# A fused trunk layer on one core: the DeltaNet scan's steps in another order on all engines, and prompt attention with paired value products and four buffers of turned weights

## The chip, the cores and the metric

The kernel is one program on one core of a Trainium2 chip. The engines are TensorE (PE, with its weight loads shown as PEld), VectorE (DVE), ScalarE (ACT), GpSimd (POOL) and SyncE (SP), which here only issues transfers. The metric is the time of one execution in device microseconds. Everything is float32, or float32 split into a rounded part and a rest (names with `hi` and `lo`).

## What is computed

One layer for two groups of frames: a prompt of 1024 frames and a sample of 32 frames of a running stream, model width 1024. Cut from the reference:

```python
def gated_delta_rule(q, k, v, g, beta, s0):        # 8 heads of 64, blocks of 64 positions
    ...
    a_mat = jnp.where(strict, jnp.einsum('nbhid,nbhjd->nbhij', kb, kc) * decay, 0.0)
    sol = lax.linalg.triangular_solve(a_mat + jnp.eye(l, dtype=a_mat.dtype), rhs,
                                      left_side=True, lower=True, unit_diagonal=True)
    ...
    def step(s, xs):
        v_new = u_i - jnp.einsum('bhld,bhde->bhle', w_i, s)
        o = (jnp.einsum('bhld,bhde->bhle', q_i * jnp.exp(g_i)[..., None], s)
             + jnp.einsum('bhij,bhje->bhie', qk_i, v_new))
        s = (s * jnp.exp(g_last)[..., None, None]
             + jnp.einsum('bhld,bhle->bhde', k_i * jnp.exp(g_last[..., None] - g_i)[..., None], v_new))
        return s, o

def stick_breaking_block(q, k, v, q_pos, k_pos):   # 8 heads of 64, queries in blocks of 128
    z = jnp.einsum('bqhd,bshd->bhqs', q, k).astype(jnp.float32) * SB_SCALE
    log_keep = jnp.where(valid, jax.nn.log_sigmoid(-z), 0.0)
    log_rest = lax.cumsum(log_keep, axis=3, reverse=True) - log_keep
    a = jnp.where(valid, jnp.exp(jax.nn.log_sigmoid(z) + log_rest), 0.0)
    return jnp.einsum('bhqs,bshd->bqhd', a.astype(v.dtype), v)
```

Before these stand a norm and one input projection, with a short convolution on the DeltaNet columns; after them an output projection, a squared-ReLU MLP of width 4096, and a gated embedding.

## The kernel before

The stages follow each other: projections; prompt attention (from about 430 us of the span to 615); attention of the 32 sample frames over a cache of 2048 (to 648); the DeltaNet scan (to 919); then the output projection, MLP and embedding, which are dense products on PE. Every engine has an instruction order written out by hand in its own block, and waits on counted semaphores. An engine never skips a waiting instruction, so the order in each block is a part of the schedule.

**Prompt attention** runs 64 steps `y`: four pairs of heads, eight blocks of 128 queries, two heads (`u`) of the pair. A step's width is 128 x (block number + 1) keys, 128 to 1024. For step `y` PE makes `scores`, ACT `sigmoids` (two passes), DVE a running product from the right (`tensor_tensor_scan`, L1544) and a product (L1545), PE turns the weights block by block (`turn_weights`, L1941), ACT copies them out of PSUM into `turned_buf` (`copy_weights`, L1146), and PE multiplies them with the values (`values`, L1954). Before, `values(y)` uses 128 value columns as the stationary operand for each head although a head needs 64, so half of each result is not used; two halves, one of each head, are then copied and split by two ACT instructions (`round_out`, L1139) and two DVE instructions (`rest_of_out`, L1533) of 64 partitions. At step `y` the order on PE is `scores(y+3)`, `turn_weights(y+1)`, `values(y)`, and on ACT `sigmoids(y+3)`, `copy_weights(y+1)`, `round_out`.

**The scan** handles 9 chunks `q`: chunk 0 is the sample (one block of 64 positions), chunks 1 to 8 are 128 prompt frames each (two blocks `g`). For each chunk, without the state: the squares and norms of q and k (`squares`, `square_sums` L2116, `logs`, `inverse_norms`, `unit_norms` L1593), the decay matrices (`raw_differences` and `decays` on POOL, `decay_differences` L1585 on DVE, `decays` on ACT), the key and query products (`key_products`, `query_products`, L2125, drained by `key_matrix` and `query_matrix`), and the inverse of the triangular matrix. This inverse starts with the 16x16 diagonal blocks: `at_out` writes the matrix to DRAM (before, `blocks_out`), `lanes_in` reads its diagonal blocks back with one block per partition, DVE inverts all of them at once (`lanes_begin`, `lanes_middle`, `lanes_end`, L1642 and L1646), SP writes them to DRAM twice (`lanes_out`, L768 and L769) and reads them back in matrix form (`t_in` L774, `x_in_blocks` L779; before, all four in `blocks_in`). PE then joins them to 32 and 64 (`first_matrices` L2219, `first_inverse` L2227 and L2233, `second_matrices`, `second_inverse`), with ACT copies between (`first_masks`, `first_blocks`, `second_masks`, `second_blocks`). The part with the state is a chain for each block: `keys_on_state` (L2163), `rest_of_values`, `solved_values` (L2172), `new_values`, `state_change` (L2181), `new_state`, and beside it `outputs` (L2193, L2197). The output is squared, summed, normed, gated, turned (`turn_outputs`, L2208), rounded and split.

Each engine has a loop over `i` in which it handles several chunks at different stages. Before, `first_matrices(i+1)` stands right behind `keys_on_state(i, 0)` on PE, the lanes of chunk `i+2` stand between the two state steps of chunk `i` on DVE, and SP waits inside `blocks_in` and `blocks_out` for one transfer to land before it issues the next. `heads_part` puts parts of the first output tile into the last iterations.

SP's `sums_in`, `conv_qk_in`, `conv_v_in` and `z_in` load a chunk's decays, q and k, v, and gate. `split_ring` on POOL splits the dense stages' weight blocks.

## Time and profile before

| | |
|---|---|
| median of 3 runs | 1903.82 us (1903.76 to 1904.57) |
| profiled execution | 1903.72 us, of it span 1902.0 us |
| PE busy | 1738.7 us, 91% of the span |
| DVE busy | 767.2 us, 40% |
| ACT busy | 502.4 us, 26% |
| POOL busy | 615.0 us, 32% |
| mean granted TensorE clock | 0.962 |

Busy time of PE is the time in which at least one matrix product was under way; it says little of how full the array was. The granted clock is a share of 2.4 GHz: 1.00 is 2.4 GHz, 0.50 is 1.2 GHz, and a number between is a mean over time.

### The profile page before, as it was taken

The page shows a single profiled execution, that of the slowest core. Times are in us where ns is not written, and L with a number is a line of the kernel's source. Part 1 is how long each engine was busy: PE and PEld are TensorE (multiplying, and loading weights), DVE is VectorE, ACT ScalarE, POOL GpSimd, SP SyncE. Part 2 cuts the span into 40 slices and gives each one's busy share as a digit, 9 for nine tenths or more (in the row PEclk, how much of TensorE's full clock was granted, in tenths as well). Part 3 has the DMA queues.
Part 4 walks back from the last instruction along what each step waited for, and adds up shares of the span by engine and source line. Part 5 has one row for each costly group of instructions (what it writes and reads, how often), then busy time and mean ns, then how long its engine had stood idle before and what let it go on. Part 6 is the DMA issues. An engine that isn't in the chain of part 4 may idle for free.

```text
span 1902.0 us, 33199 instructions
## 1 busy us (share of the span) xinstructions
PE 1738.7 (91%) x14512; PEld 1648.3 (87%) x14512; DVE 767.2 (40%) x988; ACT 502.4 (26%) x970; POOL 615.0 (32%) x340
## 2 busy tenths in 40 slices
PE   4999999997999756776999999999999999999998
PEld 4989989995777446666999999999999999999898
DVE  5552134547998455664125222122212222216422
ACT  5222103226776533342113101010100000003211
POOL 4231331322332022212433434343434444432520
PEclk9999999998999878787999999999999999999999
DMA  5112321114000534333231111111111111112211
GB/s 173 46 46 68 105 63 59 68 57 131 1 1 1 155 83 98 86 64 79 65 89 45 45 45 45 45 45 45 46 54 45 45 45 45 45 45 68 56 56 48
DMA packets 202662, 116.50 MB, mean 61 GB/s; under 512 B 74448, under 2 KB 196764, under 8 KB 202524
## 3 DMA queue, kind: packets, MB, share of 16 engines
q1 hardware_dynamic: 193024, 101.45, 18.9%
q10 hardware_dynamic: 9500, 13.02, 1.9%
q8 instruction: 111, 1.82, 0.4%
q14 instruction: 27, 0.22, 0.0%
HBM read 92.60 MB, written 21.84 MB: 60 GB/s over the span
## 4 chain that ended last, share of the span: by engine, by line
PE 73%; DVE 13%; DMA 4%; issue 4%; ACT 2%; SPq 2%; POOL 1%; ACTq 0%; DVEq 0%; POOLq 0%
PE psum L2090 42%; PE psum L1902 8%; PE psum L2376 5%; DVE act_lo_plain L1544 3%; PE psum L1871 3%; PE psum L1872 3%; PE psum L1873 3%; DVE act_hi_plain L1545 2%; DVE area L1642 1%; DMA area<-x_scratch 1%; DMA x_scratch<-area 1%; PE psum L1954 1%; PE psum L2395 1%; DVE area L1482 1%; DVE area L1646 1%
## 5 line engine op out<-in xcount | busy, mean ns | idle before, releaser
L2090 PE MATMUL psum<-act_hi,w_round 128*128 128x352 f32 x1920 | 367.6, 324 | 0.3 <-DVE act_lo L1774 0.3
L940 POOL TENSOR_TENSOR w_round<-w_plain,ones 128x1024 fp32r<-128x1024 f32 x80 | 175.6, 2194 | 508.4 <-DMA w_plain<-in_w_up_dram 227.8
L2090 PEld LDWEIGHTS psum<-act_hi,w_round 128*128 128x128 f32 x1920 | 319.8, 188 | 1.3 <-DVE act_lo L1774 0.6
L2090 PE MATMUL psum<-hid_hi,w_round 128*128 128x352 f32 x1344 | 257.5, 323 | 0.4 <-DVE hid_lo L1804 0.4
L2090 PEld LDWEIGHTS psum<-hid_hi,w_round 128*128 128x128 f32 x1344 | 222.4, 188 | 0.7 <-DVE hid_lo L1804 0.7
L1781 DVE TENSOR_TENSOR area<-psum,area 128x1056 f32<-128x1056 f32 x72 | 90.5, 1257 | 307.6 <-PE psum L2090 307.6
L2090 PE MATMUL psum<-act_lo,w_round 128*128 128x352 f32 x960 | 206.7, 323 | 0.0
L941 POOL TENSOR_TENSOR w_round<-w_plain,w_round 128x1024 fp32r<-128x1024 f32 x80 | 197.7, 2472 | 6.3
L1401 ACT ACTIVATE hid_hi<-area 128x1056 fp32r<-128x1056 f32 x28 | 30.4, 1087 | 589.1 <-DVE area L1797 589.1
L1871 PE MATMUL psum<-w_round,act_hi 128*128 128x256 f32 (+1 forms) x576 | 165.8, 288 | 6.8 <-POOLq L890 3.6
L2090 PEld LDWEIGHTS psum<-act_lo,w_round 128*128 128x128 f32 x960 | 163.2, 188 | 0.0
L1872 PE MATMUL psum<-w_round,act_hi 128*128 128x256 f32 (+1 forms) x576 | 163.1, 283 | 0.0
L1873 PE MATMUL psum<-w_round,act_lo 128*128 128x256 f32 (+1 forms) x576 | 162.0, 281 | 0.0
L2090 PE MATMUL psum<-hid_lo,w_round 128*128 128x352 f32 x672 | 143.9, 323 | 0.0
L1797 DVE SCALAR_TENSOR_TENSOR area<-psum,area 128x1056 f32<-128x1056 f32 x32 | 40.2, 1258 | 239.6 <-PE psum L2090 234.7
L887 POOL TENSOR_TENSOR w_round<-w_plain,ones 128x2048 fp32r<-128x2048 f32 x14 | 50.5, 3610 | 256.1 <-PE psum L1873 165.3
L2090 PEld LDWEIGHTS psum<-hid_lo,w_round 128*128 128x128 f32 x672 | 113.8, 188 | 0.0
L1871 PEld LDWEIGHTS psum<-w_round,act_hi 128*128 128x128 f32 (+1 forms) x576 | 104.0, 181 | 8.4 <-ACTq L1067 4.0
L1902 PE MATMUL psum<-act_hi,w_round 128*128 128x352 f32 x576 | 109.1, 324 | 0.0
L1873 PEld LDWEIGHTS psum<-w_round,act_lo 128*128 128x128 f32 (+1 forms) x576 | 104.4, 181 | 0.5
L1872 PEld LDWEIGHTS psum<-w_round,act_hi 128*128 128x128 f32 (+1 forms) x576 | 103.9, 180 | 0.5
L1544 DVE TENSOR_TENSOR_SCAN act_lo_plain<-act_lo_plain,w_plain 128x128 f32<-128x128 f32 (+7 forms) x64 | 88.3, 1380 | 24.2 <-ACT act_hi_plain L1133 14.2
(295 smaller groups left out, 2705.7 us busy)
## 6 DMA issues: line engine op xcount, KB each, us to landing
w_plain<-in_w_up_dram SPq DMA_DIRECT2D x32, 512.0 KB, 4.0
w_plain<-in_w_down_dram SPq DMA_DIRECT2D x32, 512.0 KB, 3.4
w_plain<-in_w_in_dram SPq DMA_DIRECT2D x14, 1024.0 KB, 5.4
conv_scratch<-area ACTq DMA_DIRECT2D x12, 512.0 KB, 2.7
area<-in_x_prompt_dram SPq DMA_DIRECT2D x8, 512.0 KB, 3.6
w_plain<-in_cache_k_dram SPq DMA_DIRECT2D x4, 1024.0 KB, 5.3
w_plain<-in_w_out_dram SPq DMA_DIRECT2D x8, 512.0 KB, 5.6
w_plain<-in_x_prompt_dram SPq DMA_DIRECT2D x8, 512.0 KB, 4.8
```

Of the source, the lines that this page charges most:

```text
L887: own.link(pool.tensor_tensor(hi, w_raw[:, slot, :], ones[:, 0:1].to_broadcast([P, BLK]), ALU.mult))
L940: own.link(pool.tensor_tensor(hi, ring_raw(n), ones[:, 0:1].to_broadcast([P, RB]), ALU.mult))
L941: pool.tensor_tensor(lo, ring_raw(n), hi.bitcast(F32), ALU.subtract).then_inc(ring_split, 1)
L1544: own.link(dve.tensor_tensor_scan(back, back, starts, 0.0, ALU.mult, ALU.max))
L1781: dve.tensor_tensor(h3, chunks_of(bank_set(tile)), h3, ALU.add).then_inc(drained, 1)
L1797: dve.scalar_tensor_tensor(out=by_chunk(wide[:, n % 2, :]), in0=chunks_of(bank_set(tile)), scalar=0.0, in1=by_chunk(wide[:, 2, :]), op0=AL ...
L1871: pe.matmul(out, hi[:, k, cols], w_h(k), start=(k == 0), stop=False)
L1872: pe.matmul(out, hi[:, k, cols], w_l(k), start=False, stop=False)
L1873: last = pe.matmul(out, lo[:, k, cols], w_h(k), start=False, stop=(k == K - 1))
L1902: last = pe.matmul(bank(base + c)[0:rows, 0:CH], w(k), a[:, k, CH * c:CH * (c + 1)], start=(k == 0 and w is lhs_hi and a is hi), stop=(k = ...
L2090: last = pe.matmul(bank(bank_set(tile) + c)[:, 0:CH], w(k), a(k)[:, CH * c:CH * (c + 1)], start=(begins and k == ks[0] and w is w_h and a ...
L2376: last = pe.matmul(bank(c)[:, 0:CH], w(k), a[:, k, CH * c:CH * (c + 1)], start=(k == 0 and w is w_h and a is act_hi), stop=(k == KT - 1 an ...
```

## The change

In prompt attention `values` is called once for two steps. For each block of keys it makes two products, one for each head, each with 64 value columns as the stationary operand, into the lower and the upper 64 partitions of one 128x128 result. `round_out` and `rest_of_out` become one instruction of 128 partitions each. `turned_buf` has four buffers in place of two; the new ones lie in `w_plain` where `d_cqk` and `d_gb` of the scan lie, so `conv_qk_in(0)` and `sums_in(0)` are issued after the last value product of the stage.

In the scan the order of the steps in all five loops is new. Per chunk every engine has the same instructions as before. The lanes are handled one iteration earlier against the state steps (chunk `i+3` in DVE's iteration `i`, chunk `i+2` before), SP's two long helpers are cut into five that are interleaved, and `outputs(i, 1)` stands before `state_change(i, 1)`. Of the diff, the removed loops are left out (the listing above has them):

```diff
-        turned_buf = (act_hi_plain[:, DEEP * TP:(DEEP + 1) * TP], act_lo_plain[:, DEEP * TP:(DEEP + 1) * TP])
+        turned_buf = (act_hi_plain[:, DEEP * TP:(DEEP + 1) * TP], act_lo_plain[:, DEEP * TP:(DEEP + 1) * TP],
+                      w_plain[:, 2 * BLK:2 * BLK + TP], w_plain[:, 2 * BLK + TP:2 * BLK + 2 * TP])
         q_stage = carve(area, tok0 + 2 * SW + 2 * TP + 5 * P, 2, P)
...
             conv_v_in(1)
             sp.wait_ge(consts_made, 5)
             for scratch in (at_all, x_all, t_all):
                 sp.dma_start(scratch, zeros).then_inc(scratch_cleared, 16)
             sp.wait_ge(g_stored, 16)
-            sums_in(0)
             sp.wait_ge(kc_turned, 2)
             cache_keys_in(2)
+            sp.wait_ge(o_ready, 1 + STEPS // 2)
+            conv_qk_in(0)
+            sums_in(0)
             sp.wait_ge(kc_turned, 4)
             cache_keys_in(3)
...
                 sp.wait_ge(z_stored[u], 16 * NTT)
             sp.dma_start(d_sin[:, 0], state_of["in"]).then_inc(s_loaded, 16)
 
...
+            def at_out(q):
                 sp.wait_ge(at_made, q + 1)
                 for u in range(2):
                     sp.dma_start(at_scratch[u, 0:HD, 0:mats(q)], d_at[HD * u:HD * (u + 1), q % 3, 0:mats(q)])\
                       .then_inc(at_dumped, 16)
+
+            def lanes_in(q):
                 sp.wait_ge(at_dumped, 32 * (q + 1))
                 if q:
                     sp.wait_ge(scattered, 32 * q)
                 sp.dma_start(d_lane[:, 0:LB * LB].rearrange("l (r c) -> l r c", c=LB), at_lanes).then_inc(gathered, 16)
 
...
+            def lanes_out(q):
                 sp.wait_ge(lanes_made, q + 1)
+                if q:
+                    sp.wait_ge(blocks_back[(q - 1) % 2], 64 * ((q - 1) // 2 + 1))
                 sp.dma_start(t_lanes, d_lane_t.rearrange("l (r c) -> l r c", c=LB)).then_inc(scattered, 16)
                 sp.dma_start(x_lanes, d_lane[:, 0:LB * LB].rearrange("l (r c) -> l r c", c=LB)).then_inc(scattered, 16)
+
+            def t_in(q):
                 sp.wait_ge(scattered, 32 * (q + 1))
                 if q >= 2:
                     sp.wait_ge(m_ready, level(q - 2, 1))
                 for u in range(2):
                     sp.dma_start(d_t[HD * u:HD * (u + 1), q % 2, 0:mats(q)], t_scratch[u, 0:HD, 0:mats(q)])\
                       .then_inc(blocks_back[q % 2], 16)
+
+            def x_in_blocks(q):
                 if q >= 3:
                     sp.wait_ge(vn_ready, steps_to(q - 3))
                 for u in range(2):
                     sp.dma_start(d_x[HD * u:HD * (u + 1), q % 3, 0:mats(q)], x_scratch[u, 0:HD, 0:mats(q)])\
                       .then_inc(blocks_back[q % 2], 16)
...
+            def at(q):
+                return 0 <= q < CHUNKS
+
+            for i in range(-3, CHUNKS + 1):
+                if i >= -1 and at(i + 2):
+                    sums_in(i + 2)
+                if at(i):
+                    t_in(i)
+                if at(i + 1):
+                    lanes_in(i + 1)
+                if at(i):
+                    x_in_blocks(i)
+                if i == CHUNKS - 1:
+                    for done in (kg_made, qg_made, qry_ready, kv_turned, cn_made):
+                        sp.wait_ge(done, CHUNKS)
+                    for n in range(DN_RING, RING):
+                        ring_in(n)
+                if at(i - 1):
+                    if i == 1:
                         sp.wait_ge(consts_made, 6)
...
+                    z_in(i - 1)
+                if i == 3:
                     sp.wait_ge(s_new, 2)
                     sp.dma_start(state_of["sample"], d_sin[:, 1]).then_inc(s_stored, 16)
...
+                if i >= -2 and at(i + 3):
+                    conv_qk_in(i + 3)
+                if at(i + 1):
+                    lanes_out(i + 1)
+                if at(i + 2):
+                    at_out(i + 2)
+                if i >= -1 and at(i + 3):
+                    conv_v_in(i + 3)
...
+            def at(q):
+                return 0 <= q < CHUNKS
+
+            for i in range(-2, CHUNKS + 1):
+                if at(i + 2):
+                    raw_differences(i + 2)
+                if at(i - 1):
+                    decay_state(i - 1, 0)
+                if at(i - 1) and i > 1:
+                    decay_state(i - 1, 1)
+                if at(i + 2):
+                    decays(i + 2)
+                if at(i + 1):
+                    decayed_keys(i + 1)
+                if i >= CHUNKS - 2:
...
                 act.activation(sig_buf[:, n, 0:w], z, ACT.Sigmoid, scale=HD ** -0.5).then_inc(sig_made, 1)
 
             def round_out(t):
-                act.wait_ge(o_ready, 1 + 2 * t + 2)
+                act.wait_ge(o_ready, 1 + t + 1)
                 k, cols = WT + t // NT, slice(P * (t % NT), P * (t % NT + 1))
-                for u in range(2):
-                    last = act.activation(act_hi[half(u), k, cols], bank(6 + t % 2)[half(u), P * u:P * (u + 1)], ACT.Copy)
-                last.then_inc(o_rounded, 1)
+                act.activation(act_hi[:, k, cols], bank(6 + t % 2)[:, 0:P], ACT.Copy).then_inc(o_rounded, 1)
 
             def copy_weights(y):
                 w = P * (y % UNITS // 2 + 1)
                 act.wait_ge(att_turned, 1 + y + 1)
-                act.wait_ge(o_ready, 1 + earlier(y, 2))
-                act.activation(turned_buf[y % 2][:, 0:w], psum[:, 4:6, :].rearrange("p b c -> p (b c)")[:, 0:w],
+                if y >= 4:
+                    act.wait_ge(o_ready, 1 + y // 2 - 1)
+                else:
+                    act.wait_ge(dense_ready, NC)
+                act.activation(turned_buf[y % 4][:, 0:w], psum[:, 4:6, :].rearrange("p b c -> p (b c)")[:, 0:w],
                                ACT.Copy).then_inc(att_placed, 1)
 
             for y in range(DEEP):
...
                 act.activation(rs, rs, ACT.Exp, scale=-0.5).then_inc(norms_made, 1)
 
             def last_decays(q):
-                act.wait_ge(diff_made, q + 1)
+                act.wait_ge(dtb_made, 2 * q + 1)
...
                     act.wait_ge(qt_made, q - 1)
+                    act.wait_ge(kd_made, q - 1)
+                act.wait_ge(diff_made, q + 1)
                 act.activation(d_dt[:, q % 2, 0:mats(q)], d_db[:, 0:mats(q)], ACT.Exp).then_inc(dt_made, 1)
...
+                return 0 <= q < CHUNKS
+
+            for i in range(-4, CHUNKS + 1):
+                if at(i):
+                    second_blocks(i)
+                if at(i - 1):
+                    output_norms(i - 1)
+                if at(i + 1):
+                    turned_values(i + 1)
+                if at(i + 2):
+                    last_decays(i + 2)
+                if at(i + 3):
+                    logs(i + 3)
+                if at(i + 1):
                     first_masks(i + 1)
...
+                if at(i + 3):
+                    inverse_norms(i + 3)
+                if at(i + 2):
+                    state_decays(i + 2)
+                if at(i + 3):
+                    decays(i + 3)
+                if at(i + 1):
                     first_blocks(i + 1)
...
+                if at(i + 4):
+                    squares(i + 4)
+                if at(i - 1):
+                    rounded_output(i - 1)
+                if at(i + 1):
                     second_masks(i + 1)
...
+                if at(i):
+                    output_squares(i)
             act.wait_ge(s_stored, 32)
...
-                for u in range(2):
-                    last = dve.tensor_tensor(act_lo[half(u), k, cols], bank(6 + t % 2)[half(u), P * u:P * (u + 1)],
-                                             act_hi[half(u), k, cols].bitcast(F32), ALU.subtract)
-                last.then_inc(o_split, 1)
+                dve.tensor_tensor(act_lo[:, k, cols], bank(6 + t % 2)[:, 0:P], act_hi[:, k, cols].bitcast(F32),
+                                  ALU.subtract).then_inc(o_split, 1)
...
+            def at(q):
+                return 0 <= q < CHUNKS
+
+            for i in range(-4, CHUNKS):
+                if i > 0:
                     new_state(i, 1)
...
+                if at(i):
+                    output_sums(i)
+                if at(i + 1):
+                    rest_of_values(i + 1, 0)
+                if at(i + 3):
+                    query_matrix(i + 3)
+                if at(i):
+                    normed_output(i)
+                if at(i + 1):
+                    new_values(i + 1, 0)
+                if at(i + 4):
+                    decay_differences(i + 4)
+                if at(i):
+                    gated_output(i)
+                if at(i + 3):
+                    lanes_begin(i + 3)
+                if at(i + 1):
+                    new_state(i + 1, 0)
+                if at(i + 3):
+                    lanes_middle(i + 3)
+                if at(i + 4):
+                    unit_norms(i + 4)
+                if at(i + 3):
+                    lanes_end(i + 3)
+                if at(i + 1) and i >= 0:
+                    rest_of_values(i + 1, 1)
+                if at(i + 4):
+                    key_matrix(i + 4)
+                if at(i + 2):
+                    first_transposed(i + 2)
+                if at(i + 1) and i >= 0:
+                    new_values(i + 1, 1)
+                if at(i + 3):
                     decayed_queries(i + 3)
...
-            def values(y):
-
-
-                i, u, t = y // UNITS, y % 2, y // 2
-                pe.wait_ge(att_placed, 1 + y + 1)
-                if u == 0:
-                    pe.wait_ge(o_split, 1 + max(t - 1, 0))
+            def values(t):
+
+                i = t // NT
+                pe.wait_ge(att_placed, 1 + 2 * t + 2)
+                pe.wait_ge(o_split, 1 + max(t - 1, 0))
                 for n in range(t % NT + 1):
                     rows = P - 1 if n == t % NT else P
-                    last = pe.matmul(bank(6 + t % 2)[:, P * u:P * (u + 1)], v_tok[0:rows, n, P * i:P * (i + 1)],
-                                     turned_buf[u][0:rows, P * n:P * (n + 1)], start=(n == 0), stop=(n == t % NT))
+                    for u in range(2):
+                        first = P * i + HD * u
+                        last = pe.matmul(bank(6 + t % 2)[half(u), 0:P], v_tok[0:rows, n, first:first + HD],
+                                         turned_buf[(2 * t + u) % 4][0:rows, P * n:P * (n + 1)], start=(n == 0), stop=(n == t % NT))
...
                 pe.wait_ge(qt_made, q + 1)
+                pe.wait_ge(vn_made, n + 1)
                 if q:
                     pe.wait_ge(on_read, q)
                 for k in range(WT):
...
+                last_ks, final = i == CHUNKS - 2, i == CHUNKS - 1
+                if at(i + 1):
                     first_inverse(i + 1)
...
+                if at(i) and i > 0:
                     keys_on_state(i, 1)
                 if final:
+                    heads_part([WT + 2], False)
+                if at(i - 1):
+                    turn_outputs(i - 1)
+                if at(i + 3):
+                    key_products(i + 3)
+                if at(i + 2):
+                    turn_keys(i + 2)
+                if at(i) and i > 0:
+                    solved_values(i, 1)
+                if final:
+                    heads_part([WT + 3], False)
+                if at(i + 1):
+                    second_matrices(i + 1)
+                if at(i) and i > 0:
+                    outputs(i, 1)
+                    state_change(i, 1)
+                if at(i + 1):
+                    second_inverse(i + 1)
+                    keys_on_state(i + 1, 0)
+                if last_ks:
+                    pe.wait_ge(m_made, level(i + 1, 1))
+                    pe.wait_ge(qt_made, CHUNKS)
+                    pe.wait_ge(x_made, level(i + 1, 1))
+                    heads_part([WT], True)
+                if at(i + 3):
+                    query_products(i + 3)
+                if at(i + 1):
+                    solved_values(i + 1, 0)
+                if last_ks:
                     heads_part([WT + 1], False)
...
+                if at(i + 4):
+                    square_sums(i + 4)
+                if at(i + 2):
+                    first_matrices(i + 2)
+                if at(i + 1):
+                    state_change(i + 1, 0)
+                    outputs(i + 1, 0)
             def turn_x(m):
                 pe.wait_ge(x_loaded[0], 16 * (NTT // 3) + 16 * (m + 1))
                 if m:
```

## Rows read from the trace of the kernel before

**Rows 1.** The page: granted TensorE clock in 40 slices of 47.6 us, in tenths.

```profile
PEclk9999999998999878787999999999999999999999
```

**Rows 2.** Windows of the prompt attention; window, its length, then busy time of each engine.

```profile
482.40:525.05 42.65, 41.02 (x264) 31.57 (x265) 38.93 (x49) 32.76 (x70) 15.75 (x17) 1.00 0.01 2
525.05:568.00 42.95, 41.18 (x264) 31.59 (x264) 39.23 (x49) 31.36 (x65) 16.62 (x17) 1.00 0.00 1
...
439.00:482.40 43.40, 35.39 (x201) 27.02 (x201) 35.76 (x36) 28.54 (x47) 7.80 (x11) 0.88 0.36 114
```

**Rows 3.** Groups by shape in 430 to 625: busy us, mean ns, idle before.

```profile
L1533 DVE TENSOR_TENSOR act_lo<-psum,act_hi 64x128 fp32r<-64x128 f32 x64 | 18.5, 289 | 7.2 <-ACT act_hi L1139 6.0
```

**Rows 4.** Timeline of the attention: start, duration, instruction, in brackets idle before it.

```profile
467.60 2.02 DVE L1544 TENSOR_TENSOR_SCAN act_lo_plain<-act_lo_plain,w_plain 128x896 f32<-128x896 f32 x1 [2.39 <-ACT act_hi_plain L1133]
...
525.98 1.95 PE L1954 MATMUL psum<-act_hi_plain,area 128*128 128x128 f32 x16
...
526.18 1.02 ACT L1146 ACTIVATE act_lo_plain<-psum 128x1024 f32<-128x1024 f32 x1 [0.96 <-PE psum L1941]
...
529.09 0.69 DVE L1544 TENSOR_TENSOR_SCAN act_lo_plain<-act_lo_plain,w_plain 128x256 f32<-128x256 f32 x1 [0.83 <-ACT act_hi_plain L1133]
...
531.42 0.69 DVE L1544 TENSOR_TENSOR_SCAN act_lo_plain<-act_lo_plain,w_plain 128x256 f32<-128x256 f32 x1 [1.18 <-ACT act_hi_plain L1133]
```

**Rows 5.** Timeline of the cache attention, PE: products into parts of the partitions.

```profile
620.68 1.08 PE L2011 MATMUL psum<-act_hi_plain,y_sample_t 128*64 128x512 f32 x4
...
626.04 0.65 PE L2039 MATMUL psum<-w_plain,act_hi_plain 128*32 128x64 f32 x32
```

**Rows 6.** The chain that ended last, in the scan: start, duration, what.

```profile
689.48 0.61 SPq L768
...
762.60 0.60 DVE area L1585
...
764.04 0.45 DVE area L1642 x2
...
769.98 0.60 SPq L768
...
775.24 3.15 DMA area<-x_scratch
...
778.43 2.00 PE psum L2219 x32
...
786.35 0.47 PE psum L2193 x16
...
787.28 1.91 PE psum L2116 x4
...
880.04 0.60 SPq L768
...
918.15 0.70 DVE act_lo L1725
```

**Rows 7.** Waits of the SP queue in 680 to 880: us in total, times, longest.

```profile
SPq L768 <- DVE w_plain L1678: 63.0, 7, 10.2
```

**Rows 8.** Windows of the scan, columns as in rows 2, then clock and DMA share.

```profile
734.73:844.51 109.78, 80.06 (x1926) 71.85 (x1928) 65.34 (x145) 42.54 (x97) 21.91 (x20) 0.78 0.38 85
...
771.00:772.50 1.50, 0.00 (x0) 0.00 (x0) 1.50 (x3) 0.00 (x0) 0.00 (x0) 0.96 0.64 73
...
784.50:786.00 1.50, 1.50 (x34) 1.50 (x34) 0.39 (x1) 0.28 (x2) 0.00 (x0) 0.50 0.73 156
786.00:787.50 1.50, 1.50 (x43) 1.43 (x41) 1.07 (x4) 0.79 (x3) 0.60 (x1) 0.99 0.54 132
```

**Rows 9.** Timeline of one cycle of the scan, DVE and the SP queue.

```profile
772.01 1.20 DVE L1593 TENSOR_TENSOR area<-w_plain 128x1024 f32<-128x1024 f32 x1
...
804.83 1.27 SPq L758 DMA_DIRECT2D at_scratch<-area  x2
...
810.41 2.14 SPq L671 DMA_DIRECT2D w_plain<-decay_scratch  x2
```

147 lines of the change are left out of this document (13 added, 134 removed).

## The prediction

> **What bounds the kernel now.** I read the page's slices first. The granted clock is at 2.4 GHz nearly everywhere and lower only in slices 10 to 20, which are the two stages of this change and the one between them [rows 1]. The rest is dense product work that the diff does not touch, so I price only these stages and let everything behind them move up.
>
> *Prompt attention.* Its four groups of 16 steps take 43 us each. In a window of one group PE is busy 41.0 to 41.2 us and DVE 38.9 to 39.3 us [rows 2]: both are nearly full, and ACT at 31 to 33 us is not. The chain of waits and the timeline say who is last where. Inside a group DVE runs without a gap; at the change from width 1024 back to 128 DVE idles, and the last two idle pieces are 0.83 and 1.18 us while ACT and PE are late [rows 4]. A group therefore costs DVE's own work and some 3 us of stall. The first group has a third kind of time: 2.39 us in which DVE waits while PE is behind at the lower clock [rows 4], and busy sums of 35 us in 43 [rows 2].
>
> *The scan.* The chain is one repeated cycle. DVE's decay differences and lanes (762.60 to 769.98), SP's issues and transfers to x landing at 778.39, then PE's first matrices, inverse and the rest of its queue, until DVE may go on [rows 6]. From the lanes of chunk 1 done (689.48) to those of chunk 8 (880.04) there are seven cycles: 190.6 / 7 = 27.2 us each. In four cycles of 109.78 us the busy sums are 80.1 for PE (at a mean clock of 0.78), 65.3 for DVE, 42.5 for ACT and 21.9 for POOL [rows 8]: per cycle DVE has 16.3 us of work, ACT 10.6, POOL 5.5. No engine is full; the cycle is set by latency. SP waited 63.0 us in seven times for the lanes to be made [rows 7], and PE has nothing to do in 771.0 to 772.5 [rows 8].
>
> **Attention, part by part.** (a) `rest_of_out`: two instructions of 289 ns become one. An instruction's 128 columns stay the same, so I take 289 ns for the new one and save 0.31 us with the gap, for each pair of steps [rows 3]. Where DVE is last (seven of the eight in a group) this counts: 2.2 us a group. The one at the group's change lies in DVE's idle time. `round_out` saves as much on ACT, which is not last.
> (b) `values`: 8 key blocks of one head now take 16 instructions in 1.95 us, with 0.17 us of it latency, so 0.22 us a block [rows 4]. The new form has as many products, each with 64 columns in one half of the array. Do both halves run at once? Two products of 512 columns into different halves, 4 instructions, took 1.08 us in the cache attention, where one 128-column block costs 0.22 us and one after the other would be 8 x 0.22 = 1.8 us; 32 instructions in four column parts took 0.65 us [rows 5]. So they overlap fully, and a pair's values cost half: 36 blocks x 0.22 = 8 us less PE work in each group, 41 down to 33. Bounds: 0 and 8 us. PE then stops being last even at width 1024.
> The Trainium skill ("TensorEngine Tiling (Array Packing)", Key Properties) speaks against this: changing the tiling mode drains TensorE, and here each pair of steps now changes to halves and back. Row and rule can both hold, since the 1.08 us contains such a start [rows 5]. If each change cost as much as that start's 0.2 us, 16 changes in a group would be 3 us of PE, 36 in place of 33, still below DVE.
> (c) Order at the group's change. After step 15's weights are turned, PE no longer makes `values(14)` (1.95 us at 525.98) before the next scores. ACT's copy of 1.02 us, which starts at 526.18 [rows 4], is now what stands before the sigmoids of step 18; the sigmoids of step 19 wait for scores behind one paired `values` of 1.8 us in place of two of 1.8. Following both queues, the scan at 531.42 comes at about 530.1: 1.3 us less. The four buffers let `copy_weights` run on without the values, which it needs for this.
> (d) Moved: `conv_qk_in(0)` and `sums_in(0)`, three issues of about 0.6 us, go behind the last values and into the cache attention, between two cache loads that wait for PE anyway. The scan needs them some 30 us later. Nothing; without that cover, 2 us.
> Sum: three groups x 2.2 + three changes x 1.3 + first group (1.9 in DVE's instructions and the 2.39 us in which PE was behind) + 0.5 at the end (one paired product after the last turn where 3.6 us of two overlapped with a copy) = 15.3 us. With PE not relieved it is about 2.
>
> **The scan, part by part.** Instruction counts per chunk are the same, so only order and waits matter. I wrote down each engine's new queue for one iteration and followed it at full clock. Two loops compete.
>
> *The state loop with DVE's queue.* Six hops through PE (16 instructions start to start 0.47 us [rows 6], with about 0.25 us until the result can be read) and six through DVE of 0.42 us, with what stands between them. From `new_state(i,1)`: keys, rest of values, solved values, new values, then PE has `square_sums` (1.91 us [rows 6]) and `first_matrices` (0.93) before `state_change`: 6 us to `new_state(i+1,0)`. Then DVE has the middle and end of the lanes and `unit_norms` (1.20 us [rows 9]): the lanes are 769.98 - 764.04 less one `new_values` of 0.42 = 5.5 us [rows 6], so 6.8 us with gaps. Then rest of values, key matrix, first transposed, new values 2.8 us, PE's outputs and state change 1.6 us, new state 0.5. Together 17.7 us. DVE's bare work is 16.3 us [rows 8].
>
> *The lanes' loop through SP.* From lanes done: `lanes_out` 1.3 us, `at_out` 1.27 (804.83), `conv_v_in` 0.6, `sums_in` which waits for this chunk's decayed queries and so starts at 3.6, 1.3 (I take the short end; a full queue showed 2.14), `t_in` 1.27 as `at_out`, `lanes_in` 0.6, `x_in_blocks` with its second issue at 7.5, and x 3.15 us later at 10.6 [rows 6, 9]. Here the waits for a landing that SP sat out before are covered by other issues, the transfer of the diagonal blocks among them. Behind it `first_matrices` 1.0, `state_change` and latency 0.8, `new_state` 0.5: 12.9. And `new_state(i+1,0)` stands before `lanes_middle` in DVE's queue, 6.8 us: 19.7 us. This loop is the longer one. DVE's wait for it is about 2 us a cycle; behind that wait are the lanes, and behind these SP. I add 0.8 us for slower landings when transfers crowd (they share the same bytes in 20 us instead of 27): cycle 20.5 us, bounds 17.7 and 24.
>
> *Clock.* PE's work at full clock is, from 0.47 us for 16 instructions and 1.91 for the square sums [rows 6], about 15.3 us a cycle. The clock left the upper level in a window with no PE work (771.00, 0.96) and was at 0.50 still at 784.50 [rows 8]. A set of 32 took 2.00 us there against 0.93 at full clock [rows 6]. In the new queue the longest hole I find is 2 us, before `first_matrices`, so I take full clock. The Trainium skill ("TensorE: Matmul & The Clock Gate", Part 1) says the slow state is the default and activity lifts it, and the trace agrees: 0.96 falling in a window without PE work, 0.99 after a full one [rows 8].
>
> *Start and end.* The pipeline is deeper by one, but at the start the same round trips limit it: lanes of chunk 1 done at about 690, as before; then, without state work, 17 us and 18.5 us: chunk 3 at 725.5. Five cycles of 20.5: chunk 8 at 828, against 880.04. From there before took 918.15 + 0.7 - 880.04 = 38.8 us to the last split [rows 6]. After: 12.9 to `new_state(7,0)`, 6.4 to `new_state(7,1)`, 12.5 for the two blocks of chunk 8 with the four `heads_part`s between (1.6 us each), 6 for the output: 38, and I take 40. End 868 for 918.9: 51 us less. Added waits (`vn_made` before `outputs`, `kv_turned` and `kd_made`) are met long before at this cycle. POOL's first two ring splits (about 4.5 us each) stand before `decay_state` of chunks 7 and 8 but end before these are needed.
>
> **Sum.** The profiled execution took 1903.72 us, 1.72 beside its span, and the median is 0.1 above. 1903.8 - 15.3 - 51 = 1837.5; I say 1838 us.
>
> **The rivals.**
> - *Halves do not overlap.* PE stays at 41 us a group and bounds attention; only some 2 us are gained there: 1851. Against it [rows 5].
> - *The clock stays mixed in the scan and landings are slow.* Cycle 24 us, five cycles 17.5 us more and the tail 4 more: 1859.5. For it: the start of the scan has holes anyway, and a mean of 0.78 before [rows 8].
> - *The lanes' loop is shorter than I think* (SP's issues overlap more, x lands early), cycle 17.7 by the state loop: 14 us less, 1824.
> - *Slower: TensorE stays at 1.2 GHz through the whole scan.* Its work of 15.3 us then doubles to 30.6 a cycle and PE is the bound: five cycles x 10.1 = 51 us more, the start 12 and the tail 18 more (both mostly PE's hops at the double time): 1919. It makes the kernel slower from a cycle of about 28 us on, with start and tail so. Against it: from 784.50 PE was busy for all of a window at the low level, and the next window has 0.99 [rows 8]; a full PE at the low level is what preceded the rise.
> - *The queues lock one iteration further apart* (SP's wait for `cn_made` or `kv_turned` stands before lanes it should send), so the cycle stays at 27 and only attention gains: 1888.
>
> **How the numbers follow.** Forecast (1828 to 1848) 0.58; halves apart 0.07; mixed clock 0.15; short loop 0.11; cycle unchanged 0.04; slower 0.04; and 0.01 for no difference. A difference of 0.2% (3.8 us) is about what a measurement of this kernel can tell from none. The range 1822 to 1870 holds the first four but for their edges, and the upper end lies between the mixed clock and the unchanged cycle. Faster 0.95, same 0.01, slower 0.04.
>
> **What the new profile would show.** Groups of attention at 39.5 us with PE busy near 33; L1533's successor x32 at about 289 ns; paired `values` at width 1024 in about 1.9 us. In the scan, lanes done every 20.5 us, PE's granted clock above 0.95, DVE busy over 80% of a cycle, its longest wait before `new_state` for PE, and SP without the long wait for the lanes. It would be wrong if DVE's wait stands elsewhere (at `lanes_begin` for the diagonal blocks, or at `unit_norms`), if the windows show a clock near 0.5, or if the cache attention grew by the moved loads.

## The result, and the profile after

| | median us | lowest to highest | span of the profiled run |
|---|---|---|---|
| before | 1903.79 | 1902.37 to 1904.57 | 1902.0 |
| changed | 1859.8 | 1856.62 to 1864.9 | 1861.1 |

The ratio is 0.977 (95%: 0.9753 to 0.9787). The kernel is faster by 44 us where 66 were forecast: the direction is right and the forecast gain half as large again as the measured one. The time is within the range, but outside the 1828 to 1848 us that had the chance of 0.58. Ratios here and below leave out a disturbed execution, of which there was one: 5921.7 us in run 4, whose median of 1854.6 us counts it (1854.1 without it).

Timeline of the changed kernel: the memset with which the scan clears its matrices, the first lane store of chunks 3 and 8, and the last split (start, duration, instruction).

```profile
642.73 0.53 POOL L960 MEMSET area<- 128x512 f32 x1
...
728.48 0.60 SPq L772 DMA_DIRECT2D t_scratch<-w_plain  x1
...
835.22 0.60 SPq L772 DMA_DIRECT2D t_scratch<-w_plain  x1
...
877.13 0.69 DVE L1754 TENSOR_TENSOR act_lo<-psum,act_hi 128x512 fp32r<-128x512 f32 x1 [2.70 <-ACT act_hi L1344]
```

The same memset before:

```profile
648.80 0.52 POOL L946 MEMSET area<- 128x512 f32 x1
```

Before, the scan ended at 918.85 [rows 6]. So everything ahead of the scan gave 6.1 us (15.3 forecast), and the scan shrank from 270.1 to 235.1 us: 35 us (51 forecast). Its cycle is (835.22 - 728.48) / 5 = 21.35 us against 27.4 for the same five cycles before (27.2 is the mean of seven); I had said 20.5.

Windows of the changed kernel, with the columns of [rows 2] and [rows 8]: two groups of the attention, then the scan's five cycles from chunk 3 to 8.

```profile
480.58:520.62 40.04, 35.74 (x251) 23.38 (x252) 35.44 (x41) 29.67 (x60) 15.55 (x16) 0.97 0.00 1
520.62:561.97 41.35, 37.18 (x266) 24.77 (x264) 35.64 (x42) 28.50 (x56) 13.37 (x16) 0.95 0.01 1
...
728.48:835.22 106.74, 86.27 (x2384) 77.42 (x2384) 85.82 (x179) 50.70 (x116) 30.34 (x25) 0.92 0.46 97
```

In the attention both full engines lost work, as worked out: DVE from 39 to 35.5 us, PE from 41 to 36 or 37. But a group still takes 40.0 and 41.35 us, and the clock, 1.00 before, is now 0.97 and 0.95. In the scan DVE is busy for 80% of a cycle: 17.2 us, not the 16.3 of [rows 8], though it has the same instructions; runs 6 and 10 below show why.

Timeline of PE at a group's change.

```profile
517.88 1.30 PE L1977 MATMUL psum<-ident,act_hi_plain 128*128 128x128 f32 x8 [1.94 <-ACT act_lo_plain L1165]
519.11 0.48 PE L1990 MATMUL psum<-act_hi_plain,area 128*64 128x128 f32 x1
...
519.38 0.42 PE L1990 MATMUL psum<-act_hi_plain,area 128*64 128x128 f32 x1
...
522.17 0.49 PE L1969 MATMUL psum<-area 128*128 128x128 f32 x2
...
524.97 1.97 PE L1990 MATMUL psum<-w_plain,area 128*64 128x128 f32 x32
```

The last row is the paired product of width 1024: 32 instructions in 1.97 us, where 16 took 1.95 [rows 4]. The halves overlap fully. The first rows show what eats the gain: PE stands 1.94 us for ACT's copy, comes back to a falling clock (0.50 from 519 to 521; a product of one half takes 0.42 us, not 0.27), and the scores of the next group's second step (L1969 at 522.17) stand 3.1 us behind a paired product at that clock. At the change one group earlier PE stands as long, but the clock stays at 1.00. The rows are that wait and DVE's second scan of the group, at this earlier change and at the one above.

```profile
477.84 1.06 PE L1977 MATMUL psum<-ident,act_hi_plain 128*128 128x128 f32 x8 [1.94 <-ACT act_lo_plain L1165]
...
481.52 0.42 DVE L1569 TENSOR_TENSOR_SCAN act_lo_plain<-act_lo_plain,w_plain 128x128 f32<-128x128 f32 x1 [0.19 <-ACT act_hi_plain L1151]
...
523.17 0.42 DVE L1569 TENSOR_TENSOR_SCAN act_lo_plain<-act_lo_plain,w_plain 128x128 f32<-128x128 f32 x1 [1.81 <-ACT act_hi_plain L1151]
```

So a fall of the clock there costs DVE 1.6 us of waiting.

The chain that ended last, one cycle of the scan (start, duration, what).

```profile
750.34 0.61 SPq L772
...
758.28 3.49 DMA area<-x_scratch
...
761.81 1.17 PE psum L2257 x32
...
763.01 0.36 ACT area L1307
...
764.51 1.07 ACT w_plain L1277
...
765.66 1.22 DVE w_plain L1619
766.88 1.81 DVE area L1668
768.71 0.69 DVE area L1672
769.43 1.36 DVE area L1668
...
771.91 0.60 SPq L772
```

It closes in 21.57 us: SP's issues 7.9, x's landing 3.5, PE's first matrices 1.2, ACT's first masks and then its inverse norms 2.6, DVE's norms and the end of the lanes 6.3. It does not pass through the state at all. Three of the five cycles close so; in the fourth SP holds the issue of x until PE has made `solved_values` (801.46), and the fifth closes through `state_change` and `new_state`. And two products of the same form take 1.81 and 1.36 us where each took 1.0 to 1.1 before.

### The profile page after: what moved, and what is told of

The parts are those of the page before. It is cut to its first block, busy times and chain, and to the rows that moved or that the text cites. A ratio compares the mean times of both kernels' runs of the same rounds, so it can differ in the third digit from the quotient of the medians.

```text
span 1861.1 us, 33169 instructions
## 1 busy us (share of the span) xinstructions
PE 1715.9 (92%) x14512; PEld 1612.1 (87%) x14512; DVE 772.6 (42%) x956; ACT 492.9 (26%) x938; POOL 610.9 (33%) x340
## 4 chain that ended last, share of the span: by engine, by line
PE 77%; DVE 8%; issue 5%; ACT 4%; SPq 3%; DMA 3%; POOL 1%; ACTq 0%; DVEq 0%; POOLq 0%
PE psum L2127 44%; PE psum L1938 8%; PE psum L2419 5%; PE psum L1907 3%; PE psum L1908 3%; PE psum L1909 3%; PE psum L1969 2%; PE psum L1977 2%; PE psum L1990 2%; DVE area L1668 2%; DMA area<-x_scratch 1%; PE psum L2438 1%; DVE area L1509 1%; DVE act_lo L1810 1%; DVE area L1672 1%
## 5 line engine op out<-in xcount | busy, mean ns | idle before, releaser
L954 POOL TENSOR_TENSOR w_round<-w_plain,ones 128x1024 fp32r<-128x1024 f32 x80 | 169.8, 2122 | 512.2 <-DMA w_plain<-in_w_up_dram 227.1
L955 POOL TENSOR_TENSOR w_round<-w_plain,w_round 128x1024 fp32r<-128x1024 f32 x80 | 204.3, 2554 | 6.3
```

Of the source, the lines that this page charges most:

```text
L954: own.link(pool.tensor_tensor(hi, ring_raw(n), ones[:, 0:1].to_broadcast([P, RB]), ALU.mult))
L955: pool.tensor_tensor(lo, ring_raw(n), hi.bitcast(F32), ALU.subtract).then_inc(ring_split, 1)
```

## The experiments

Each ran beside the kernel before on the same chip; before's median was 1902.6 to 1904.0 us there. The changed kernel was not run again beside them. "Group" is the second group of the attention, from its first scan to the next group's; "scan" runs from the memset to the last split; "cycle" is the mean of the five from chunk 3 to 8. All three are from the profiled run.

| kernel | median us | ratio, 95% | group | scan | cycle |
|---|---|---|---|---|---|
| before | 1903.8 | | 42.75 | 270.1 | 27.4 |
| changed | 1859.8 | 0.9753-0.9787 | 40.04 | 235.1 | 21.35 |
| 1 attention alone | 1892.2 | 0.9935-0.9977 | 39.80 | 265.5 | 26.6 |
| 2 scan alone | 1871.5 | 0.9816-0.9849 | 42.75 | 236.4 | 21.44 |
| 3 halves apart | 1877.5 | 0.9845-0.9878 | 46.31 | 236.5 | 21.71 |
| 4 values later | 1854.6 | 0.9720-0.9758 | 39.03 | 235.5 | 21.55 |
| 5 x first | 1856.3 | 0.9723-0.9761 | | 228.1 | 20.81 |
| 6 keys apart | 1858.4 | 0.9744-0.9776 | | 231.2 | 20.99 |
| 7 norms first | 1862.7 | 0.9755-0.9793 | | 236.4 | 21.68 |
| 8 = 4 + 5 + 6 | 1843.3 | 0.9661-0.9694 | 39.04 | 226.9 | 20.35 |
| 9 = 8, filled | 1844.8 | 0.9665-0.9704 | | 227.4 | 20.85 |
| 10 = 8, decays apart | 1854.6 | 0.9727-0.9760 | | 233.8 | 21.76 |
| 11 = 8, stores by ACT | 1843.2 | 0.9673-0.9706 | | 225.0 | 20.28 |
| 12 = 9 + 11 | 1848.4 | 0.9693-0.9729 | | 230.8 | 21.63 |

The changed kernel's own runs lie 8 us apart, so single steps of 1 to 4 us are read from the stages, not from the medians.

**1 and 2. Each part alone.** The kernel before with the diff's attention part, and with its scan part.

> The attention part of the change alone; the scan's five loops are those of before. Reading of the changed kernel's trace (the stage ends 6 us earlier, because TensorE, relieved of half its value products, falls to 1.2 GHz at each group's change): 1897.5 us, -6. The prediction's own term: -15 us, 1888.5. If the two parts only gain together: no difference.

> The scan part alone, attention as before. Reading of the trace (scan 235.5 us in place of 270.5): -35 us, 1869 us, the lanes of two chunks 21.4 us apart. The prediction's term: -51 us, 1853, 20.5 us apart.

By the medians the attention gives 11.4 us (4.4 to 12.4 by the ratio's interval) and the scan 32.1 (29 to 35), together 43.5 of the 44: within these intervals the parts add. Both gave less than forecast: 15 us are outside the attention's interval, the 6 us read from the trace are in it. The attention's number is loose: the ten runs lie between 1887.1 and 1905.7 us, and the profiled one is the fastest. In it the stage ends 12.3 us earlier than before, not 6.1, and the scan, whose code is that of before, is 4.6 us shorter.

**3. Halves one after the other.** All of one head's key blocks, then the other's.

```
-                for n in range(t % NT + 1):
-                    for u in range(2):
+                for u in range(2):
+                    for n in range(t % NT + 1):
```

> The changed kernel with the value products of a pair of steps in another order: first all key blocks of one head, then all of the other, so that no two neighbouring products use different halves of the array. If the halves' overlap is what makes a pair cost 1.97 us at width 1024, a pair now takes about 3.7 us, PE's work in a group rises from 33 to 41 us, and the stage is as long as before or longer, since the products now stand in one piece before the next scores: +6 to +12 us on the changed kernel (1866 to 1872). If the halves also overlap across a distance or the overlap is worth nothing to the stage: no difference, 1860.

Timeline of PE: the same 32 instructions as at 524.97 above.

```profile
532.23 3.33 PE L1990 MATMUL psum<-w_plain,area 128*64 128x128 f32 x32
```

3.33 us against 1.97, both at a granted clock of 1.00, and a group of 46.3 us against 40.0. The time is 17.7 us longer than the changed kernel's, where 6 to 12 were expected. What halves the cost is that the two halves of the array alternate instruction by instruction; half-width products alone would have made the kernel slower in this stage than before.

**4. Values later.** The paired values of steps y-2 and y-1 stand behind the scores of y+3, so at a group's change PE has work while it waits for ACT's copy, and the new group's scores go ahead of the old group's values.

```
                 scores(y + DEEP)
+                if y and y % 2 == 0:
+                    values(y // 2 - 1)
                 turn_weights(y + 1)
...
-                if y % 2:
-                    values(y // 2)
```

> The changed kernel with PE's order at an even step y: scores(y+3), the value products of steps y-2 and y-1, turn_weights(y+1). So they fill the time in which PE waited for ScalarE's copy, and never wait for a copy themselves. If the group's change is slow because PE waits for the copy with nothing to do, falls to 1.2 GHz and then has 3 us of values before the next scores: groups at 39 to 40 us in place of 40 to 41.4, the clock near 1.00, -5 us (1855). Rival: what is last there is ScalarE's own queue (copy of 1.02 us before the next sigmoids) and PE's order is without weight: no difference (1860).

Windows: the same two groups.

```profile
479.51:518.54 39.03, 35.26 (x265) 22.71 (x266) 35.98 (x41) 30.25 (x60) 12.88 (x16) 1.00 0.01 1
518.54:557.59 39.05, 35.27 (x265) 22.72 (x266) 35.99 (x42) 29.39 (x56) 12.88 (x16) 1.00 0.01 1
```

The clock is 1.00 again and the groups take 39.0 us, half a microsecond under the forecast. From the second group to the memset it takes 154.6 us, not 162.2. The stage ends 14.7 us earlier than before, where 15.3 were forecast. So the missing gain of the attention lay at the groups' changes. The first change above, at the full clock, is followed by a group of 40.0 us and the second, after a fall, by one of 41.35: 1.3 us go with the clock's fall, and the last 1.0 us down to run 4 are left for PE's standing and its order.

**5. x first.** SP issues a chunk's x ahead of the next lane load, and V's load behind both.

```
                     t_in(i)
-                if at(i + 1):
-                    lanes_in(i + 1)
                 if at(i):
                     x_in_blocks(i)
+                if at(i + 1):
+                    lanes_in(i + 1)
+                if i >= 0 and at(i + 2):
+                    conv_v_in(i + 2)
```

> SyncE alone is changed in the changed kernel: the load of a chunk's x blocks goes out before the next chunk's lane loads, and the load of V's convolution inputs goes behind both instead of ahead of the lanes' store. Theory (the lanes' loop through SyncE's queue sets the cycle of the scan): x lands about 1.2 us earlier (the two issues of 0.6 us ahead of it are gone), so the cycle from chunk 3 to chunk 8 falls from 21.35 us to 20.1 to 20.4 us, and the kernel takes 7 to 9 us less than the changed one, some 1851 us. Rival (the loop is bound by the state's chain or by VectorE's own work, SyncE's share of it has slack): the cycle stays within 0.2 us of 21.35 and the time within 2 us of 1860.

The scan is 7.0 us shorter, but the cycle fell by 0.5 and not by 1.0 to 1.2 us: 3.9 us came ahead of chunk 3's lanes. The median is only 3.5 us below the changed kernel's, of 7 to 9 expected. In this run's chain two cycles, from 704 and from 746 us, no longer pass through x but through the state's products and the square sums; groups of 16 take 1.05 us there, 0.47 at the full clock. Two others wait in SP's queue for DVE's decayed queries.

**6. Keys apart.** POOL scales a chunk's keys only after DVE made its lanes.

```
                 if at(i + 1):
+                    pool.wait_ge(lanes_made, i + 2)
                     decayed_keys(i + 1)
```

> GpSimd waits until VectorE has made the lanes of the chunk before it scales that chunk's decayed keys, so that the two no longer run beside each other; nothing else is changed. Theory (two engines that work in SBUF at once slow each other, and that stretches the lanes in the loop): the two long 64x512 steps of the lanes fall from 1.80 and 1.35 us to 0.95 to 1.15 us, the cycle falls by 0.7 to 1.2 us and the time by 5 to 8 us. Rival A (their length comes from something else): they stay at 1.35 to 1.8 us and the time at 1860. Rival B (the decayed keys, 2 us later, are now late for the state): the lanes get shorter but the cycle does not, or grows by up to 1 us.

Timeline of DVE's lanes and of POOL, first the changed kernel, then this one.

```profile
766.69 1.09 POOL L976 TENSOR_TENSOR area<-area,nbeta 128x512 f32<-128x512 f32 x1 [1.91 <-ACT area L1295]
766.80 1.88 DVE L1668 TENSOR_TENSOR area<-area 64x512 f32<-64x512 f32 x1
767.75 2.07 POOL L984 TENSOR_TENSOR area<-area,w_plain 128x512 f32<-128x512 f32 x1
...
769.43 1.34 DVE L1668 TENSOR_TENSOR area<-area 64x512 f32<-64x512 f32 x1
```

```profile
765.04 1.27 POOL L976 TENSOR_TENSOR area<-area,nbeta 128x512 f32<-128x512 f32 x1 [1.51 <-ACT area L1296]
765.32 1.88 DVE L1669 TENSOR_TENSOR area<-area 64x512 f32<-64x512 f32 x1
...
767.95 1.09 DVE L1669 TENSOR_TENSOR area<-area 64x512 f32<-64x512 f32 x1
...
770.24 1.27 POOL L984 TENSOR_TENSOR area<-area,w_plain 128x512 f32<-128x512 f32 x1 [3.93 <-DVE w_plain L1705]
```

The second product fell from 1.34 to 1.09 us and the keys from 2.07 to 1.27, but the first stayed at 1.88. Read as turns taken, this fits: whichever began later stands until the other has ended. The decays begin at 766.69 and end at 767.78; the product that begins at 766.80 stands for that 1 us, and runs in the rest. The keys, begun at 767.75, stand until it ends at 768.68. The Trainium skill ("SBUF — State Buffer", SBUF: two separate sides) says as much: DVE with two operands in SBUF and POOL share a pair of ports under an exclusive lock. Run 10 tests it. The kernel before had the same exclusion, but there GpSimd began later and paid, 1.61 us for an operation that takes 1.04 alone (run 10):

```profile
765.95 1.02 DVE L1642 TENSOR_TENSOR area<-area 64x512 f32<-64x512 f32 x1
...
766.28 1.61 POOL L962 TENSOR_TENSOR area<-area,nbeta 128x512 f32<-128x512 f32 x1 [6.59 <-ACT area L1274]
```

The scan gained 3.9 us, the cycle 0.36: half of the least that the theory said (0.7 to 1.2). The median gained 1.4 us, of 5 to 8 expected.

**7. Norms first.** ACT's inverse norms ahead of its first masks.

> ScalarE makes the inverse norms of the lanes before the masks of the first matrices; its order alone is changed. Theory (the loop through ScalarE's masks ends only 0.24 us after the loop through the state's change, so taking it away gives that much): the cycle falls by 0.2 to 0.3 us, the time by 1 to 2 us, near what can be told. Rival (ScalarE's four masks are the whole of what the cycle has too much): the cycle falls by 1.2 to 1.5 us and the time by 8 to 10 us. A third way: the masks, 1.1 us later, hold up TensorE's first inverse, and the cycle grows by up to 1 us.

No gain: the scan is 1.3 us longer and the cycle 0.3, both within what profiles of the same scan code differ by (runs 2, 3 and 4 and the changed kernel: 235.1 to 236.5 us, 21.35 to 21.71). The rival (ACT's masks are the whole excess) is out; the 0.2 us of the theory can't be told. DVE no longer waits for the norms' inputs, but its waits for PE's `state_change` stay, 10.9 us in eight times (10.7 before this edit).

**8. Three edits together** (4, 5 and 6).

> Three edits together in the changed kernel: the paired values behind the next scores (1854.6 us alone in the run before), x ahead of the lane loads on SyncE, and GpSimd's decayed keys behind the lanes. If all three theories hold and their gains add, 1854.6 less 7 to 9 and less 5 to 8: 1838 to 1843 us. If the scan is bound elsewhere, 1853 to 1856 us. If the decayed keys become late, 1856 to 1862 us.

1843.3 us: at the upper edge of what full addition of the expected gains would give, and 16 us under the changed kernel. It is more than the 10 us that the three medians gained alone; by the stages the attention gave 9.5 us and the scan 8.2. It is the best version found; run 11 equals it.

**9. TensorE filled.** In the changed kernel and in run 8 a part of the state's chain runs at the lower clock in most cycles. Windows of run 8: its five cycles, and a part of the state's products in one of them.

```profile
714.67:816.41 101.74, 86.16 (x2384) 77.26 (x2384) 81.11 (x179) 50.49 (x116) 21.53 (x23) 0.92 0.48 102
...
760.85:764.00 3.15, 3.15 (x74) 2.97 (x72) 2.07 (x4) 0.97 (x3) 0.00 (x0) 0.50 0.58 148
```

Two more copies of V's 32 turns stand where PE was idle before them (same values into the same place, the signal on the last).

```
+                turn_values_again(q)
...
                     solved_values(i, 1)
+                if at(i + 2):
+                    turn_values_again(i + 2).then_inc(kv_turned, 1)
```

> The three edits of the run before (1843.3 us) and, in the scan, work for TensorE that changes no result: V's 32 turns of a chunk are made three times instead of once, the second time right behind the first and the third behind the second half's solved values, where TensorE stood for 1.2 and 1.0 us. It adds 64 matmuls (2.2 us of TensorE at the full clock) to each chunk. Theory (the clock falls to 0.50 for some 3 us of each chunk because TensorE stands before the state's chain, and that chain, which takes twice as long then, lies in the loop): the granted clock stays at 1.00 through the chain, the values' and outputs' groups of 16 take 0.47 us in place of 0.85, the cycle falls from 20.35 us to 18.3 to 19.3 us and the time by 8 to 16 us. Rival A (the clock falls all the same, or the half clock is not in the loop): the cycle grows by 0 to 1 us and the time by 0 to 8 us. Rival B (TensorE's queue is full, so that 2.2 us more of work count): the cycle grows by 1 to 2 us.

```profile
714.05:818.32 104.27, 90.64 (x2706) 81.62 (x2701) 82.69 (x179) 50.68 (x116) 22.56 (x23) 0.98 0.48 100
```

The clock rose from 0.92 to 0.98, the cycle did not fall (20.85), and between 728 and 816 us PE's waits for x grew from 4.1 us in two times to 7.6 in four. Rival A holds: what the full clock gives, PE then stands and waits for x. The fill also adds 2.2 us of PE work to a cycle, and this run can't tell its price from the clock's gain.

**10. Decays apart.** POOL's decays behind the keys too, so no POOL product runs beside the lanes.

> The three edits (1843.3 us) and GpSimd's decays moved behind the decayed keys as well, so behind VectorE's lanes. Theory (an operation of VectorE on two operands in SBUF and one of GpSimd exclude each other, and whichever began later stands until the other has ended; the first long step of the lanes begins 0.1 us after the decays): the first long step falls from 1.88 us to 1.03 us, like the second one did from 1.34 to 1.08 when the decayed keys were moved. The lanes end 0.85 us earlier, but the decays now come 5 to 6 us later, behind which VectorE's key matrix stands for 2 to 3 us, so the time is 1842 to 1850 us. Rival (the first step is long for a reason of its own, its operands' strides): it stays at 1.8 to 1.9 us.

```profile
757.24 1.02 DVE L1669 TENSOR_TENSOR area<-area 64x512 f32<-64x512 f32 x1
...
759.01 1.09 DVE L1669 TENSOR_TENSOR area<-area 64x512 f32<-64x512 f32 x1
```

The first product takes 1.02 us in every full cycle: the exclusion is shown, from both sides. As a version the run is worse than I expected, 1854.6 us with a cycle of 21.8, since the key matrix behind the decays is late: DVE stands for it 10.5 us in the five cycles, up to 2.1 at a time.

**11. The key matrix's stores by ACT.** The two issues of `at_out` leave SP's queue for ACT's, behind the rounded output.

```
-                if at(i + 2):
-                    at_out(i + 2)          # SP
...
                     rounded_output(i - 1)
+                if at(i + 3):
+                    at_out(i + 3)          # ACT
```

> The three edits (1843.3 us), and the two stores of a chunk's key matrix to the scratch go out from ScalarE's queue, behind the rounded output, where ScalarE stands for 2 us, instead of from SyncE's between the lanes' stores and the loads of the state's sums. Theory (the lanes' loop through SyncE and x sets the cycle, since the fill of TensorE to the full clock gained nothing): the issues of 0.68 and 0.67 us leave the loop, x lands 1.3 us earlier, the cycle falls from 20.35 us to 19.1 to 19.8 us and the time by 4 to 9 us, to 1834 to 1839 us. Rival A (the state's chain at the half clock closes a loop of its own of the same length): the cycle falls by less than 0.3 us, and only the next run, with the fill, gains. Rival B (ScalarE, held 1.3 us by the issues, is late with the second masks): the time grows by 0 to 8 us.

The chain that ended last, one cycle of it.

```profile
759.05 0.61 DVE area L1632
...
759.73 0.49 SPq L672
...
760.96 0.60 SPq L774
...
761.60 1.46 SPq L774
...
763.10 0.64 SPq L781
...
763.77 3.44 DMA area<-x_scratch
...
767.26 1.17 PE psum L2263 x32
```

1843.2 us and 20.28: no gain. With the stores gone, SP's load of the decays (L672) waits for DVE's decayed queries (L1632), 7.0 us in four times, and holds x as long as the stores did. I had this wait in the forecast ("waits for this chunk's decayed queries") and forgot it in this run's expectation; it is the third loop, and it already closes two cycles of run 5's chain and two of run 9's.

**12. Both.**

> The run before with V's turns three times as in the filled kernel (1844.8 us without the move of the stores). If SyncE's loop alone sets the cycle: as the run before but for 0 to 4 us more. If the two loops are of one length, so that each hides what the other gains: the cycle falls to 18.5 to 19.3 us and the time to 1828 to 1836 us, below the run before.

1848.4 us, cycle 21.6: neither of the two ways expected. The idea that two loops hide each other's gain is out in this form: with the stores moved and PE's work added, PE waits 14.0 us in five times for x (5.8 in four in run 11). In the cycle that I followed, SP held the issue of x until PE had made that chain's solved values, whose buffer x takes.

## Why the prediction was right in direction and too large

Against the profiled run 24.8 us are missing (1862.8 for 1838). By the stages: attention 9.2, start of the scan 9.0, cycle 4.2, tail 2.6, which makes 25.0.

- **Values at half the cost** (8 us of PE a group): right, 1.97 us for 32 instructions; run 3 shows the rival's world. In run 4, at the full clock, PE has 35.3 us a group for my 33. The Trainium skill's rule on drained modes ("TensorEngine Tiling (Array Packing)", Key Properties) can have cost at most these 2.3 us; 3 were worked out for it. In any case DVE's 36.0 us hide it.
- **One instruction in place of two** in `rest_of_out`: right, DVE's 39 us fell to 35.5.
- **The group's change, 1.3 us less**: this step failed, in its path and its clock. I followed the queues at full clock from the turn of step 15 on. The loss begins one turn earlier, at that of step 14 (517.88), where I did not ask what PE does while it waits for ACT's copy. Before, `values(12)` stood there:

```profile
519.55 1.73 PE L1954 MATMUL psum<-act_hi_plain,area 128*128 128x128 f32 x14
...
521.88 1.06 PE L1941 MATMUL psum<-ident,act_hi_plain 128*128 128x128 f32 x8 [0.38 <-ACT act_lo_plain L1146]
```

  Now PE stands for 1.94 us, at two of three changes the clock falls, and then 3.1 us of paired values stand ahead of the next scores (1.7 us where it stays up). Beside the 2.2 us of DVE's instructions, the second group gained 0.5 us where 1.3 were expected, and the third lost 0.6. Run 4 puts it right: groups of 39.0. The last group with the cache attention, from which I had taken 2.7 us, took 80.8 us (568.60 to 648.80 before, so 80.2) and takes 76.6 in run 4.
- **First group, 4.3 us less and 1.3 for its change**: 2.0 us here and 5.4 in run 1, with the same code. After the same 3.67 us of PE's idle time the clock fell to 0.50 here and stayed at 1.00 there. Windows of the changed kernel, then of run 1:

```profile
461.00:463.00 2.00, 2.00 (x6) 1.13 (x5) 1.97 (x3) 1.57 (x3) 0.00 (x0) 0.50 1.02 344
```

```profile
457.00:461.00 4.00, 3.64 (x29) 2.56 (x31) 3.96 (x3) 3.75 (x7) 1.31 (x1) 1.00 0.91 277
```

  The changed kernel's four runs have mean clocks of 0.972 and 0.973 at 1857 us and 0.969 at 1863 and 1865. That this one fall makes the two levels was not tried.
- **Start of the scan, 17 and 18.5 us** for chunks 2 and 3: the largest error in the scan, they took 22.1 and 21.6, and chunk 1's lanes stood 0.8 us later than I took. I had priced these cycles as free of state work. The chain of the first one closes through `state_change` and `new_state` of chunk 0, the sample:

```profile
697.79 0.88 PE psum L2218 x16
...
698.75 0.42 DVE area L1729
```

  The second closes through ACT's masks and the norms, as the cycle shown above, which no term had.
- **Cycle 20.5 us**: 21.35. The mechanism, the lanes' loop through SP, was right: x earlier helps (run 5), fill to the full clock does not (run 9). In the cycle shown x lands 11.4 us after the lanes, just as forecast (10.6 + 0.8). The way back differs: DVE's norms wait for ACT, but `new_state`, my path, ends only 0.24 us earlier, so the cycle would be nearly as long by my path.

```profile
765.66 1.22 DVE L1619 TENSOR_TENSOR w_plain<-w_plain 128x1024 f32<-128x1024 f32 x1 [0.24 <-ACT w_plain L1277]
```

  The term that was too small is the lanes with the norms, 8.0 us and not 6.8: 1.1 us of exclusion with POOL, which no term had, and these 0.24.
- **Full clock in the scan**: wrong, 0.92, but raising it gained nothing in the full cycles (run 9).
- **Tail, 40 us**: 42.6. DVE's last gated output is on the chain and began beside one of POOL's ring splits. It took 1.95 us, and 0.97 in the kernel before (0.68 in the full cycles). Changed, then before:

```profile
872.48 1.95 DVE L1748 TENSOR_TENSOR area<-area 128x512 f32<-128x512 f32 x1
```

```profile
915.29 0.97 DVE L1719 TENSOR_TENSOR area<-area 128x512 f32<-128x512 f32 x1
```

  I had asked of the splits only whether they hold up `decay_state`. The rest of the 2.6 us stays open; the clock is 0.83 in the tail.
- **The moved loads and added waits at nothing**: nothing in either profile speaks against it, and run 4 has the same loads with a last group 3.6 us shorter than before.
- **The rivals**: none of the five came in. "Mixed clock, cycle 24" is near by its time (1859.5), but by luck: its cycle did not come.

What stays open: how long the cycle of 20.3 us would be by each of the three loops (x through SP, decayed queries through SP, the state's chain) if the two others were shorter. The largest gain of a single edit was 0.54 us a cycle (run 5).

## What to carry to other kernels

When an order written by hand is tightened, look for every path by which the longest loop can close, including those that skip the work you think of as the bound; when one was shortened here, another was at most half a microsecond behind. Where a transition lets TensorE stand for 2 us, price the work behind it at both clocks (it fell at two of three such places here), and put work that is ready into that gap. And when an operation of GpSimd and one of VectorE on two SBUF operands come to run side by side, price them one after the other, on the engine that begins later.

## What the runs showed of the hardware

- VectorE's product of two SBUF operands and GpSimd's exclude each other: 1.88 and 1.34 us beside GpSimd, 1.02 and 1.09 without it; GpSimd's keys 2.07 beside and 1.27 apart. The reduction between them keeps its 0.68 us. The wait shows as a longer instruction, not as idle time.
- Products into two halves of the array overlap fully when they alternate (32 in 1.97 us) and only in small part when one half's come first (3.33 us), both at a granted clock of 1.00.
- After the same idle time of 3.67 us and with the same code, the granted clock fell in one execution and not in another. After 1.94 us it fell to 0.50 at one change of groups and stayed at 1.00 at another of the same execution.
